# Attention, output projection, norm and routing of a hybrid decoder step: three stages written as one

## The reference, cut to what matters

```
q = partial_rope(dq, pos); k = partial_rope(dk, pos)          # prompt rows; first quarter of each component
s = einsum('bqhcd,bkhcd->bhcqk', qi, k) * 64 ** -0.5          # two maps c per head, causal
p = softmax(s); w = p[:, :, 0] - lam * p[:, :, 1]
a_out = rmsnorm(einsum('bhqk,bkhv->bqhv', w, v), w_subln) * (1.0 - lam_init)
xp = xp + concatenate([g_out, a_out]) @ w_out                 # g_out: the recurrence's half
xf = rmsnorm(xp, w_norm_ffn)
g_logits = xf @ w_group; e_logits = xf @ w_expert             # 4 groups, 32 experts
# best group, its two best experts, softmax weights; then the experts and the final norm
```

## Time and profile before

| | us |
|---|---|
| median of 3 runs | 2310.84 (2307.51 to 2314.61) |
| the profiled execution, its own time | 2317.32 |
| span of its trace, first to last instruction | 2315.7 |
| mean granted clock of PE over the span | 0.861 of 2.4 GHz |

### The profile page before, as it was taken

One profiled execution on the slowest core, in us unless ns is written; L12 is line 12 of the kernel. 1 busy time (PEld: TensorE's weight loads), 2 busy tenths in 40 slices (PEclk: granted clock), 3 DMA queues, 4 the chain that ended last, 5 costly groups with the idle time before them and its releaser, 6 DMA issues. The chain is left out here.

```text
span 2315.7 us, 26776 instructions
## 1 busy us (share of the span) xinstructions
PE 1859.6 (80%) x10007; PEld 1060.6 (46%) x10007; DVE 706.9 (31%) x1698; ACT 450.6 (19%) x875; POOL 646.0 (28%) x657
## 2 busy tenths in 40 slices
PE   3999999899839888898446989959992399999980
PEld 2555533354338555563134455634441255555540
DVE  3233300000022555553273455533334011111116
ACT  3444210000021111111002233321110022222211
POOL 1255655576301323333000000000003233333313
PEclk9999999999957999998655577779985599999995
DMA  7488888898732999999535000022110798888846
GB/s 264 144 265 265 266 299 318 303 346 303 256 116 74 362 358 353 376 367 380 187 142 191 10 5 9 5 62 82 67 51 10 268 364 296 309 325 300 329 139 254
DMA packets 173744, 510.49 MB, mean 220 GB/s; under 512 B 42566, under 2 KB 64626, under 8 KB 148509
## 3 DMA queue, kind: packets, MB, share of 16 engines
q0 software_dynamic: 71536, 349.78, 40.4%
q1 hardware_dynamic: 81619, 143.33, 18.4%
q10 hardware_dynamic: 20466, 15.74, 2.1%
HBM read 556.85 MB, written 53.60 MB: 264 GB/s over the span
## 5 line engine op out<-in xcount | busy, mean ns | idle before, releaser
L206 POOL DMA_INDIRECT sd_ring<-in_cache_kT,sd_kidx x320 | 321.2, 1004 | 292.3 <-PE ps L245 172.2
L741 PE MATMUL ps<-pj_w_row,pj_xT 128*128 128x512 f32 (+1 forms) x640 | 233.7, 519 | 0.0
L2088 PE MATMUL ps<-ex_w_gu,ex_xT 128*64 128x256 f32 x2048 | 232.4, 380 | 0.0
L210 POOL DMA_INDIRECT sd_ring<-in_cache_v,sd_vidx x128 | 124.7, 974 | 375.8 <-PE ps L280 357.6
L2088 PEld LDWEIGHTS ps<-ex_w_gu,ex_xT 128*64 128x64 f32 x2048 | 147.0, 137 | 101.2 <-issue 36.3
L1741 POOL DMA_DIRECT2D scr_hn<-mx_hn x9 | 4.9, 542 | 626.9 <-DVE mx_hn L1792 626.9
L709 PE MATMUL ps<-pj_xT,pj_w_ch 128*128 128x352 f32 x576 | 177.4, 461 | 1.6 <-ACT pj_xT L519 1.6
L741 PEld LDWEIGHTS ps<-pj_w_row,pj_xT 128*128 128x128 f32 x640 | 119.9, 192 | 121.1 <-issue 113.9
L280 PE MATMUL ps<-sd_ring,sd_wT 128*32 128x512 f32 x1024 | 146.3, 651 | 31.7 <-DMA sd_ring<-in_cache_v,sd_vidx 31.7
L2110 PE MATMUL ps<-w_out,ex_hhT 128*64 128x512 f32 x512 | 124.0, 605 | 24.5 <-DVE ex_hhT L2061 24.5
L1890 PE MATMUL ps<-w_out,mx_mixT 128*128 128x512 f32 x288 | 141.6, 655 | 2.2 <-ACT mx_mixT L1754 2.2
(11 more groups left out here) (387 smaller groups left out, 2450.8 us busy)
## 6 DMA issues: line engine op xcount, KB each, us to landing
sd_ring<-in_cache_kT SPq DMA_DIRECT2D x192, 256.0 KB
scr_ys<-ex_y SPq DMA_DIRECT2D x128, 128.0 KB, 5.4
pj_w_row<-in_w_row SPq DMA_DIRECT2D x3, 2048.0 KB, 13.6
pj_w_ch<-in_w_ch SPq DMA_DIRECT2D x12, 512.0 KB, 3.5
scr_qkvT<-pj_work ACTq DMA_DIRECT2D x12, 512.0 KB, 5.9
scr_proj<-pj_work ACTq DMA_DIRECT2D x24, 256.0 KB, 2.0
gd_qkv<-scr_qkvT SPq DMA_DIRECT2D x8, 768.0 KB, 9.5
sd_ring<-in_cache_kT,sd_kidx POOLq DMA_INDIRECT x320
```

What stands on the lines that cost most here:

```text
L206: pool.indirect_dma_start(out=self.ring[:, slot, j * H * P:(j + 1) * H * P], out_offset=None, in_=self.A["cache_kT"], in_offset=bass.Indir ...
L210: pool.indirect_dma_start(out=self.ring[:, slot, :], out_offset=None, in_=self.A["cache_v"].rearrange("g (l a) c -> (g l) (a c)", a=CHUNK) ...
L741: last = pe.matmul(ps[:, 1 + g % 4, 0:w], xT[:, c, t * P:(t + 1) * P], wr[:, c, at:at + w], start=(c == 0), stop=(c == KD - 1))
L2088: last = pe.matmul(ps[i * ST:(i + 1) * ST, b, 0:2 * HF], rows[:, c, :], w_gu[:, l, c, i, :], start=(c == 0), stop=(c == KD - 1))
```

## The change

`phase_attention` and `phase_mix` become one stage, `phase_attention_mix`; the rotation moves into it, tile by tile. On PE a unit (t, h) now is: the next unit's scores, turns that are due (k, q, attention result, hn, recurrence rows), a quarter of tile t-1's projection, the turn of the unit's weights, the weighing. Both maps' scores alternate piece by piece. The turns share two banks in a fixed order, all copied by ACT. `w` is one DVE operation: it is no longer divided by the first map's sum, which enters the norm instead (`rcp`, `rho`). The attention result and the recurrence rows are turned straight into `mixT`. Tile 8 is computed on its 24 rows, its 4 heads as one unit. Slots go to the experts through SBUF: rows are placed by one-hot matmuls in place of the scatters (`in_lo`, `in_hi`), and `rows_of`, `slots` and `wt` stay in SBUF. The combine stage works on 24 rows in tile 8.

```diff
-                all_rows = A["proj"][CONV_W - 1:CONV_W - 1 + RPAD, :].rearrange("(t p) c -> p t c", p=P)
-                for dst, src in [(cos[:], A["cos"]), (sin[:], A["sin"]), (all_qk[:], all_rows[:, :, C_DQ:C_DQ + 2 * H * DV])]:
-                    sp.dma_start(dst, src).then_inc(qk_loaded, 16)
-                sp.dma_start(vals[:], all_rows[:, :, C_DV:C_DV + H * DV]).then_inc(v_loaded, 16)
...
+            def _(sp):
+                load_qk(0)
+                for dst, src in [(ident[:], A["ident"]), (cos[:], A["cos"]), (sin[:], A["sin"]), (causal[:], A["causal"]),
...
+                                 (lane_no[:], A["lane_no"]), (smp[:], A["mix"][LP:ROWS, HW:2 * HW])]:
+                    sp.dma_start(dst, src).then_inc(c_loaded, 16)
+                load_qk(1)
+                sp.dma_start(vals[:, 0:FULL, :], rows[0:SEQ, C_DV:C_DV + HW].rearrange("(t p) c -> p t c", p=P)).then_inc(v_loaded, 16)
+                sp.dma_start(vals[0:N_META, FULL, :], rows[SEQ:LP, C_DV:C_DV + HW]).then_inc(v_loaded, 16)
+                for t in range(2):
+                    load_g(t)
+                    load_x(t)
                 sp.dma_start(w_out[:], A["w_out"].rearrange("(c p) n -> p c n", p=P)).then_inc(w_loaded, 16)
+                sp.wait_ge(v_loaded, 32)
...
                 for t in range(TILES):
+                    sp.wait_ge(roped, t + 1)
+                    sp.dma_start(A["p_k"][t * P:t * P + n, :], qk[0:n, t % 2, HW:2 * HW]).then_inc(pk_stored[t % 2], 16)
+                    if t + 2 < TILES:
+                        sp.wait_ge(pk_stored[t % 2], 16 * (t // 2 + 1))
+                        sp.wait_ge(turn_ps, turn_no["Q", t] + 1)
+                        load_qk(t + 2)
+                    if 2 <= t:
+                        sp.wait_ge(turn_ps, turn_no["gdn", t - 2] + 1)
+                        load_g(t)
+                    if 3 <= t:
+                        sp.wait_ge(x2_ready, 2 * (t - 2))
+                        load_x(t - 1)
...
+            def _(act):
+                for n, (t, h) in enumerate(units[:-1]):
+                    if h == 0 and t >= 1:
+                        attended(t - 1)
+                    if h == 0 and t >= 2:
+                        square(t - 2)
...
+                    for i in range(len(groups[n])):
+                        weights(n, i)
+                    for c in range(2):
+                        exp(n + 1, c)
+                    if h == 1 and t >= 3:
+                        routes(t - 3)
...
+            def _(dve):
+                for n, (t, h) in enumerate(units[:-1]):
                     weights(n)
+                    for c in range(2):
+                        maximum(n + 1, c)
+                    if h == 0 and t >= 1:
                         norm(t - 1)
+                    if h == 0 and t >= 2:
+                        hidden(t - 2)
+                    if h == 1 and t >= 3:
+                        route(t - 3)
+                    if h == 1 and t >= 1:
+                        residual(t - 1, 0)
+                    if h == 2 and t + 2 < TILES:
+                        rope(t + 2)
+                    if h == 3 and t >= 1:
+                        residual(t - 1, 1)
...
+                def project(t, i, part):
+                    if part == 0:
+                        read("gdn", t)
+                        if t or i:
+                            pe.wait_ge(x2_ready, 2 * t + i)
+                    else:
+                        read("ao", t)
+                    for c in range(H * part, H * part + H):
+                        last = pe.matmul(ps[:, X2B, :], mixT[:, c, :], w_out[:, c, i * HALF_D:(i + 1) * HALF_D], start=(c == 0), stop=(c == KD - 1))
...
+                def project_tail():
+                    for c in range(KD):
+                        for i in range(2):
+                            last = pe.matmul(ps[32 * i:32 * i + 32, AV, :], mixT[:, c, 0:32], w_out[:, c, i * HALF_D:(i + 1) * HALF_D],
+                                             start=(c == 0), stop=(c == KD - 1))
...
+                def scores(n):
+                    if n:
+                        pe.wait_ge(e_ready, 2 * n)
+                    halves = [slice(DQ * c, DQ * (c + 1)) for c in range(2)]
                     for k0 in range(0, wd, 512):
                         k1 = min(k0 + 512, wd)
+                        for c, r in enumerate(halves):
+                            pe.matmul(flat[:, c * SCORE_C + k0:c * SCORE_C + k1], qT[r, h, t * P:(t + 1) * P], KT[r, h, k0:k1],
+                                      start=True, stop=k1 != wd, skip_group_check=True)
...
+                scores(0)
+                pe.wait_ge(v_loaded, 32)
+                pe.wait_ge(w_loaded, 16)
+                for n, (t, h) in enumerate(units[:-1]):
+                    if n + 1 < LAST:
+                        scores(n + 1)
+                    else:
+                        scores_tail()
...
+                    if t:
+                        project(t - 1, h // 2, h % 2)
                     for i in range(len(groups[n])):
+                        turn_weights(n, i)
+                    for i in range(len(groups[n])):
                         weigh(n, i)
...
+                for u in range(2 * TILES):
+                    last = pe.matmul(ps[:, 2, 0:PAIR_SLOTS], in_lo[:, u, :], in_hi[:, u, :], start=(u == 0), stop=(u == 2 * TILES - 1))
...
-                for t in range(TILES):
-                    for c in range(2):
-                        pool.indirect_dma_start(out=A["slot_tok"], out_offset=bass.IndirectOffsetOnAxis(ap=slot_i[:, t, c:c + 1], axis=0),
-                                                in_=tok[:, t:t + 1], in_offset=None).then_inc(scattered, 16)
...
-                    sp.dma_start(rows_of[:], A["slot_tok"].rearrange("(j p) o -> p (j o)", p=P)).then_inc(loaded, 16)
...
-                sp.dma_start(slots[:].rearrange("p t c -> p (t c)"), A["slots"]).then_inc(loaded, 16)
-                sp.dma_start(wt[:].rearrange("p t c -> p (t c)"), A["weights"]).then_inc(loaded, 16)
```

More of the change, by code:

```diff
@@ L1256, in _, with phase_sample_gdn @@
                 sd.on_pe(pe, UNITS_S)
-def phase_sample_gdn(nc, ps, A, keep, all_qk, vals):
+def phase_sample_gdn(nc, ps, A, keep):
     N = BS * H
@@ new lines, in _ @@
+                attended(FULL - 1)
+                square(6)
+                normed(6, 0)
+                normed(6, 1)
+                weights(LAST, 0)
+                weights(LAST, 1)
+                from_attention(7)
+                weights(LAST, 2)
+                logits(6)
+                attended(8)
+                routes(5)
+                from_recurrence(8)
+                from_attention(8)
+                square(7)
+                routes(6)
+                normed(7, 0)
+                normed(7, 1)
@@ L1537, in _ @@
+                square(8)
+                logits(7)
+                normed(8, 0)
+                routes(7)
+                logits(8)
+                routes(8)
             @block.vector
@@ new lines, in _ @@
+                hidden(6)
+                norm(7)
+                residual(7, 0)
+                route(5)
+                norm(8)
+                residual(7, 1)
+                route(6)
+                hidden(7)
+                residual(8, 0)
+                residual(8, 1)
+                hidden(8)
+                route(7)
+                route(8)
+                dve.wait_ge(rank_ps, 1)
+                ch.link(v.tensor_copy(cnt[:], ps[:, 1, 0:NE]))
+                ch.link(v.tensor_scalar(cnt_i[:], cnt[:], float(ST - 1), None, ALU.add))
@@ L1594, in _, with turn, read, key_or_query @@
-                pe.wait_ge(kT_ready, TILES)
-                pe.wait_ge(qT_ready, TILES)
-                def scores(n, c):
+                pe.wait_ge(c_loaded, 16 * 20)
+                def turn(*name):
+                    if turn_no[name] >= 2:
+                        pe.wait_ge(turned, turn_no[name] - 1)
+                    return turn_bank(*name)
+                def read(*name):
+                    pe.wait_ge(turned, turn_no[name] + 1)
+                def key_or_query(name, t):
+                    n, o = (P if t < FULL else 32), (HW if name == "K" else 0)
+                    pe.wait_ge(roped, t + 1)
+                    dst = turn(name, t)
+                    for h in range(H):
+                        last = pe.transpose(dst[:, h * n:(h + 1) * n], qk[0:n, t % 2, o + h * P:o + (h + 1) * P], ident[0:n, 0:n])
+                    last.then_inc(turn_ps, 1)
@@ new lines, in normed, with logits @@
+                def normed(t, i):
+                    n = rows_in(t)
+                    pe.wait_ge(hn_ready, t + 1)
+                    dst = turn("hn", t, i)
+                    for k, c in enumerate(range(4 * i, 4 * i + 4) if t < FULL else range(KD)):
+                        last = pe.transpose(dst[:, k * n:(k + 1) * n], hn[0:n, t % 2, c * P:(c + 1) * P], ident[0:n, 0:n])
+                    last.then_inc(turn_ps, 1)
+                def logits(t):
```

(6 more changed lines are left out.)

893 lines of the change are left out of this document (488 added, 405 removed).

## The result

The changed kernel takes 2119.49 us (median of 4 runs, 2116.58 to 2125.86) against 2309.18 before: a ratio of 0.9183, 95% interval 0.9151 to 0.9216, 190 us less. Forecast were 114 us less, 2197, with a range down to 2150.

The account below looks back on a forecast made before the run. TensorE bounds the attention and mix, small chains with DMAs the gaps. Start 36, tile 0 17, tiles 1 to 7 336 and tail 82 give 471 against 577; with 8 saved outside, 2203 profiled, 2197 us forecast, range 2150 to 2265.

Parts of the forecast that it names:

- a granted clock of 0.8: Tiles 1 to 7 of the merged stage: 205 us of PE work divided by 0.8, plus 80 of waits, 336 us.
- rival A: Merged stage: projection pieces lift the clock to 0.9 to 1.0 and nothing drops it; 2169 to 2146 us; chance 0.13.
- theory T: The experiments' first theory, not the prediction's: the dense projection piece in each head lifts the clock and holds it.
- Start and tile 0: Merged stage's beginning: 36 us of constants and queued loads, then 17 us for four heads without projection.
- PE's release by w_out: Head loop's first turned weights come 35 to 37 us after the stage's first load, released by w_out's DMA.
- The full pair (0.25 N): Tiles 1 to 7: both scores halves run together, 0.25 us per key block and head; no gain would be 0.50.
- The wait: PE's wait behind each turn for copies and exponentials: 2.0 us at t=1 to 3.5 at t=7, 80 for all heads.
- The scores' releaser: Tiles 1 to 7: PE idles before the scores 1 to 2 us a head, released by ACT's exponential.
- The tail's idle: After the last full head PE idles about 10 us, within a tail of 82 us.
- Rival D: Stage's start: the wait for w_out takes back the saved border work, costing 36 us; no chance of its own.
- Rival C: Low clock from end to end of tiles 1 to 7: 159 us more, 2356 us, slower; chance 0.05.
- Rival B: Attention's clock 0.7 (2234 us) or scores in series (2241): chance 0.20 for one; both, about 2284: 0.05.

Follow-up runs that it names:

- 3: Changed kernel with three unread copies on ACT ahead of each head's exponentials in tiles 1 to 7, lengthening PE's pauses; 2269.88 us.
- 9: Kernel before with the attention's norm on DVE cut into four parts, one behind the maxima of each head; 2275.41 us.
- 4: Kernel before with only the scores' halves paired piece by piece, issued ahead of the turn of the weights; 2241.37 us.
- 6: Changed kernel with each scores half followed by its own mask matmul, and one matmul in place of four in each projection piece; 2091.61 us.
- 5: Changed kernel with each scores half followed by its own mask matmul over 128 rows, so halves cannot run side by side; 2168.74 us.
- 2: Changed kernel with one matmul in place of four in each projection piece of tiles 0 to 7, three quarters left out; 2055.96 us.
- 10: Changed kernel with three idle copies on ACT in the second head of each tile alone, seven pauses in all; 2164.99 us.
- 11: Changed kernel with scores' halves apart, a quarter of the projection, and three idle ACT copies in each tile's second head; 2139.37 us.
- 8: Changed kernel with PE's wait for w_out moved from the head loop's start to the first projection piece; 2116.9 us, ratio 0.9139.
- 12: Changed kernel with 7 and 8, w_out's load and the values' store behind tile 2's loads, tile 7's first piece ahead of hn's turns; 2085.32 us.
- 7: Changed kernel with the projection piece behind the turn of the weights instead of ahead of it; 2096.89 us, ratio 0.906.

## Why the prediction was wrong

**The step that failed** is "I take a granted clock of 0.8, halfway between the two stages that are merged". It is 51 of the 84 us: in tiles 1 to 7 the clock was 0.99. Nothing made the mean of two old stages a price for the new one, and the reason given against rival A, "the wait of 2 to 3.5 us after each", took a wait in the chain for idle time of PE, though the same sum says that the weighing runs inside it. Counted from the same rows, the pause left was 3.5 - 2.0 = 1.5 us at eight blocks; measured 0.25 + 0.72. The run with true pauses of 3.65 us in each head (3) came to 0.81: the guess fits a stage that this one isn't.

**Why the clock is full**, as far as the runs show. Much differs from the old attention; two of the differences were varied: the pauses (the earlier trace rows holds 2.35 us of idle, behind DVE's norm, which the merged stage runs beside the projection), and the share of PE's busy time that goes to scores on 64 rows (in the table, the scores' line over the busy time of the same stretch; the line below is that of the kernel before).

```profile
L1605 PE MATMUL ps<-at_KT,at_qT 64*128 64x512 f32 (+3 forms) x240 | 130.5, 667 | 0.9 <-DVE at_qT L1544 0.9
```

| kernel | share on 64 rows | longest idle of PE | clock |
|---|---|---|---|
| before | 130.5 of 262, 50% | 2.0 to 3.4 us, six times | 0.70 |
| 9, norm spread | 123.8 of 245, 51% | 2.1 once, else under 1.3 | 0.76 |
| 4, pairs in before | 56.5 of 175, 32% | 1.7 to 2.9 a tile | 0.82 |
| 6, apart and thin | 77.6 of 211, 37% | 1.7 once | 0.94 |
| 5, apart | 76.5 of 281, 27% | 0.8 | 0.95 |
| 2, thin | 37.0 of 162, 23% | 1.3 to 2.5 a tile | 0.98 |
| changed | 37.5 of 240, 16% | 0.8 | 0.99 |

In the old stage either alone goes a part of the way at most (0.76, 0.82). In the new one the loss of either is borne: pauses like the old ones in 2, halves apart in 5 and 6. Longer pauses, of 3.4 to 3.8 us, bring the clock down there, to 0.93 (one a tile) or 0.81 (one a head). So the runs show that long pauses cost the clock, and that neither the pairs nor three quarters of the projection are needed to hold it. That it is full because less of PE's time is on 64 rows and no long pause interrupts it is argued from the table, not shown. Both changes together were never put into the kernel before, and in 9 the share on 64 rows was 53% at the low clock and 55% at the full one. Few key blocks alone don't hold it low either: in 6, heads of two and three blocks with their halves apart ran at the full clock, though with less of the time on 64 rows (6.2 of 17.9 us).

```profile
1282.00:1304.00 22.00, 17.94 (x81) 10.47 (x81) 11.81 (x40) 11.49 (x35) 0.00 (x0) 1.00 0.16 48
```

What turns the balance stays open. That the dense piece holds the clock, as rival A and theory T said, is refuted by 2 for three quarters of the piece; 10 against 11 shows that the clock is back sooner after a pause where pairs and whole pieces follow, without telling the two apart.

**The other steps.** Start and tile 0 were right to a microsecond, and PE's release by w_out stands 35.1 us after the stage's first load (35 to 37 forecast). The full pair (0.25 N) was right: undoing it in 5 cost 39 us where 35 were priced. The wait was 12 us too large in the sum (67.9 against 80). The scores' releaser is ACT's exponential, as forecast, with 0.2 to 0.8 us a head in place of 1 to 2. DVE doesn't release PE in the heads (one wait of 0.5 us). The tail's idle was 8.5 us (10), the stage's end 5 us sooner. No scatters are left on POOL, and the experts' second gather follows the first. Rival D decided nothing; moving the wait alone (8) regained 4 of its 15 us, and with the loads reordered too (12) tile 1's first piece starts 12 us sooner than in 7. Rival C lost its ground: its price assumed low clock throughout. Rival B's conditions (0.7, or scores in series) didn't come about. Two sums were off without weight: at a quarter less than 349 GB/s the start is 44 us, not 41 (24/0.75 + 12.5), and 3456 elements at L1861's rate are 3.9 us, not 4.8.

**Rule and row.** The Trainium skill ("TensorE: Matmul & The Clock Gate", A second HAM failure mode) tells of a kernel in which brief and frequent idling between groups of matmuls makes the clock swing. The trace disagrees for pauses of 0.25 to 0.8 us, two in each head (0.99), and agrees for those of 3.65 us (0.81). The Trainium skill ("TensorEngine Tiling (Array Packing)", Theoretical Speedup) gives up to twofold for a dimension of 64 or less: the trace agrees, 76.5 us against 37.5.

## What to carry to other kernels

A wait in a chain isn't idle time of the engine: subtract what the engine itself does inside it before judging its clock, and price the clock with bounds, from stretches of like work and like idle gaps, not from the mean of old stages. Put small chains (norms, exponentials) under a dense block of the busy engine, and place the block where the longest chain begins: behind the turn of the weights, not ahead of it, it took 23 us off the stage. When a wait is moved, look in which queue the next one stands.

## What the runs showed of the hardware that was not expected

- Two halves on different 64 rows run side by side whichever order they are issued in (1.99 us for both, where the earlier trace rows has 1.98 for one); a mask matmul on all rows between them ends that (76.5 us against 37.5 over tiles 1 to 7).
- PE busy 89.68 of 90 us can stay at the lower clock all the time when half of that work (47.8 us) uses 64 rows; a burst of 12 us over 128 rows raised it, and it was low again within 6 us, two us behind an idle time of 1.13 us. The same kind of heads also ran 75 us at the full clock with 55% on 64 rows.
- The same prefix of the program, unchanged, ended up to 16 us apart in the profiled executions (1209.4 to 1225.8 us), more than some of the effects looked for; stages are compared from their own first load.
